# mLSTM heads: where the turned SSD columns, the second half's scaling and the output gate's tanh stand

## What is computed

```
y_ssd = group_rmsnorm((y + d_skip * xs) * silu(z), norm_w, SSD_GROUPS)   # 2 groups of 512 columns
qk    = silu(causal_dwconv_2(qk, conv_w, conv_b))                       # 4 taps, 2048 columns
h     = num / den, per head, then normed per head                      # 8 heads of 128
y_ml  = sigmoid(o_pre) * h
x     = x + concat([y_ssd, y_ml]) @ w_out
```

## Time and profile before

| | us |
|---|---|
| median of 3 runs (1051.25 to 1052.91) | 1052.33 |
| the profiled execution, its own time | 1052.15 |
| its span, from first to last instruction | 1050.4 |
| TensorE busy | 1024.9 (98% of the span) |
| VectorE busy | 844.0 (80%) |
| ScalarE busy | 665.8 (63%) |

### The profile page before, as it was taken

The page is one execution under the profiler, slowest core; times in us unless marked ns, Lnnn a source line. Parts: engine busy times, 40 slices in busy tenths (PEclk is TensorE's granted clock), DMA queues, the critical chain, the costliest instruction groups (busy, mean ns, idle before and its releaser), DMA issues. The chain is left out here.

```text
span 1050.4 us, 14956 instructions
## 1 busy us (share of the span) xinstructions
PE 1024.9 (98%) x5574; PEld 867.9 (83%) x5574; DVE 844.0 (80%) x1091; ACT 665.8 (63%) x833; POOL 33.2 (3%) x40
## 2 busy tenths in 40 slices
PE   7999999999999999999999999999999999999997
PEld 6778999999999788989878778787878787777775
DVE  5856776766777767887868799999999999999976
ACT  5554655555565746566544677777777777777754
POOL 1001000000000100100220000000000000000000
PEclk9999999999999999999999999999999999999998
DMA  9734447464624445333204889998989898999971
GB/s 343 266 121 140 148 174 231 144 227 156 206 85 161 160 163 164 121 123 120 81 33 182 316 322 379 358 385 347 389 349 387 348 385 349 370 364 373 364 281 43
DMA packets 82712, 253.61 MB, mean 241 GB/s; under 512 B 4161, under 2 KB 42177, under 8 KB 62657
## 3 DMA queue, kind: packets, MB, share of 16 engines
q1 hardware_dynamic: 82624, 252.50, 63.9%
HBM read 251.44 MB, written 1.05 MB: 240 GB/s over the span
## 5 line engine op out<-in xcount | busy, mean ns | idle before, releaser
L1061 DVE TENSOR_TENSOR WL<-raw,WH 128x2048 fp32r<-128x2048 f32 x232 | 497.8, 2176 | 95.6 <-ACT WH L544 95.5
L544 ACT ACTIVATE WH<-raw 128x2048 fp32r<-128x2048 f32 x232 | 421.5, 1823 | 91.3 <-PE bank L1991 75.7
L1989 PE MATMUL bank<-WH,MXH 128*128 128x512 f32 x552 | 218.8, 396 | 0.2 <-DVE WL L1061 0.2
L1991 PE MATMUL bank<-WH,MXL 128*128 128x512 f32 x552 | 215.4, 390 | 0.0
L1990 PE MATMUL bank<-WL,MXH 128*128 128x512 f32 x552 | 214.9, 389 | 0.0
L1989 PE MATMUL bank<-HTH,WH 128*128 128x256 f32 x576 | 165.3, 287 | 2.4 <-DVE HTL L1084 1.2
L1990 PE MATMUL bank<-HTL,WH 128*128 128x256 f32 x576 | 162.9, 283 | 0.0
L1991 PE MATMUL bank<-HTH,WL 128*128 128x256 f32 x576 | 162.9, 283 | 0.0
L1989 PE MATMUL bank<-WH,HTH 128*128 128x512 f32 x348 | 138.6, 398 | 3.3 <-DVE WL L1108 1.5
L1990 PE MATMUL bank<-WL,HTH 128*128 128x512 f32 x348 | 136.1, 391 | 0.0
L1991 PEld LDWEIGHTS bank<-WH,MXL 128*128 128x128 f32 x552 | 103.6, 188 | 22.4
(11 more groups left out here) (393 smaller groups left out, 1097.8 us busy)
## 6 DMA issues: line engine op xcount, KB each, us to landing
raw<-in_exp_w_up SPq DMA_DIRECT2D x52, 1024.0 KB, 7.4
raw<-in_exp_w_gate SPq DMA_DIRECT2D x52, 1024.0 KB, 8.1
raw<-in_exp_w_down SPq DMA_DIRECT2D x52, 1024.0 KB, 6.8
raw<-in_w_in SPq DMA_DIRECT2D x34, 1024.0 KB, 5.1
raw<-in_w_up SPq DMA_DIRECT2D x22, 1024.0 KB, 5.4
raw<-in_w_down SPq DMA_DIRECT2D x11, 1024.0 KB, 5.2
raw<-in_w_out SPq DMA_DIRECT2D x8, 1024.0 KB, 4.9
raw<-in_w_o SPq DMA_DIRECT2D x4, 1024.0 KB, 6.6
```

The lines of the kernel that those rows point to most:

```text
L544: e.activation(WH[i % HL][:, 0:n], raw[i % RAW][:, 0:n], ACT.Copy).then_inc(a_wh, 1)
L1061: e.tensor_tensor(l, r, h.bitcast(F32), ALU.subtract).then_inc(v_wl, 1)
L1989: e.matmul(out_, ah, bh, start=start, stop=False)
L1991: return e.matmul(out_, al, bh, start=False, stop=stop)
```

## The change

- **Column parts one head later.** The four `ssd_columns(n)` stood behind heads 0 to 3 as n = h; they now stand behind heads 1 to 4 as n = h - 1, on all three engines.
- **Scaling of the second group.** VectorE's `group_norm(1)` leaves its place ahead of the head loop and goes to `turned()` of head 2, ahead of the column part there.
- **Output gate.** The two halves' tanh on ScalarE stood in heads 1 and 2; they now stand in heads 0 and 2.

```diff
@@ scalar: turned() of the head loop
                     ml_turned(h)
-                    if h < 4:
-                        ssd_columns(h)
-                    if h in (1, 2):
+                    if 0 < h < 5:
+                        ssd_columns(h - 1)
+                    if h in (0, 2):
                         e.wait_ge(a_og, 4)
-                        e.activation(OG[:, h - 1, :], OG[:, h - 1, :], ACT.Tanh, scale=0.5).then_inc(a_ogt, 1)
+                        e.activation(OG[:, h // 2, :], OG[:, h // 2, :], ACT.Tanh, scale=0.5).then_inc(a_ogt, 1)
@@ vector: ahead of the head loop
             product("mk", 0, 1)
-            group_norm(1)
             split(PI["mk", 0] + 2)
@@ vector: turned() of the head loop
-                    if h < 4:
-                        ssd_columns(h)
+                    if h == 2:
+                        group_norm(1)
+                    if 0 < h < 5:
+                        ssd_columns(h - 1)
```

## The result

The changed kernel takes 1053.44 us (median of 20 runs, 1052.45 to 1054.64), the kernel before beside it on the same chip 1051.84 us (20 runs). The ratio is 1.0014, with a 95% interval of 1.0008 to 1.0020: 1.5 us slower, inside the 0.2% that the prediction called no change, and of the sign that it forecast (+1.3 us). The profiled execution took 1053.05 us, with a span of 1051.3; that is only 0.90 us more than the profiled execution before. The two differ elsewhere too: the kernel before has a fall of the granted clock near its end (0.66 from 1025 to 1030 us) that this execution has not.

The account below looks back on a forecast made before the run. TensorE, busy 98%, was taken as the bound. Gains reach -0.80 at ml_s(2), back to -0.11 at ml_s(4), then +0.45 for the part and +0.96 wait: +1.30, 1053.45 on the execution, median 1053.6, range 1051.4 to 1054.8.

Parts of the forecast that it names:

- What bounds: mLSTM stretch: TensorE has 1.70 us at most to win, no slack after 466 us; VectorE and ScalarE loop in equal steps.
- Scaling leaves the head of the loop: VectorE ahead of head 0: split, taps and sums come 0.80 us earlier; ml_s(2) runs at 464.53, still waiting 1.35 us.
- head 2 takes it back: VectorE behind head 2's tile 1 taps: the scaling spends the 0.80 us lead; head 3's taps stay at 473.65.
- The wait at ml_y(0): TensorE in head 0, just ahead of 450.19: a 0.26 us gap that goes away.
- slower: Rival, chance 0.14: head 0 never wins the 0.80 us lead but head 2 pays it; +2.10 us, median 1054.4.
- Column part leaves head 0: Head 0: VectorE wins nothing, as the part filled a wait for ScalarE; on TensorE 0.45 us is put off, not removed.
- Tanh: ScalarE: one 1.07 us gate tanh moves from head 1 into head 0's 2.23 us idle time, at no cost.
- ml_v(4): TensorE behind head 4: waits 0.96 us for VectorE's late read of the fourth column part; runs at 490.66, 1.30 us later.
- hand over: Between the end of VectorE's column read and ml_v(4): put at 0.15 us; without any, the lower bound is +1.06.
- Not slower: Rival, chance 0.14: VectorE's idle time absorbs the scaling in head 2, the 0.80 us lead lasts; median 1052.0, or 1052.8 execution.
- The rule of the Trainium skill: Speed up the engine blocking the matmul engine: by it alone, relieving the 1.44 us gap at ml_s(2) would be a gain.
- The clock: TensorE's clock is 1.00 around the 1.44 us gap; no new wait is longer, so no drop was expected.

Follow-up runs that it names:

- gn_home_fill: The changed kernel with the second group's scaling back ahead of the head loop, plus 5 idle matmuls ahead of ml_s(2): 1053.29 us against 1052.11 before.
- after_fill: The changed kernel with 5 idle matmuls on TensorE in the gap ahead of ml_s(2): 1053.19 us against 1052.05 for the kernel before.
- part3_late: The kernel before with only the fourth column part moved from behind head 3 to behind head 4, on all three engines: 1052.78 us against 1052.05.
- read_early_fill: The changed kernel, VectorE reading the last column part ahead of head 4's tile 1 taps, plus 5 idle matmuls ahead of ml_s(2): 1052.31 us against 1052.11.
- tanh_only: The kernel before with only the gate's first tanh moved from head 1 to head 0: 1051.87 us against 1052.11.
- gn_slot_fill: The changed kernel, scaling in head 0 behind the product of tile 0, plus 5 idle matmuls ahead of ml_s(2): 1052.72 us against 1052.11 before.
- slots: The kernel before with VectorE's scaling (head 0) and column reads (heads 1 to 4) each behind the product of tile 0: 1050.76 us against 1051.61.
- gn_home: The changed kernel with the second group's scaling back ahead of the head loop: 1054.15 us against 1051.61 for the kernel before.
- read_early: The changed kernel with VectorE reading the last column part in head 4 ahead of the taps of tile 1: 1052.71 us against 1051.61 before.
- gn_slot: The changed kernel with the scaling in head 0 behind the product of tile 0: 1053.30 us against 1051.61 for the kernel before.
- the filled kernels: The kernels before and after the change, each with 5 idle matmuls on TensorE ahead of ml_s(2): 1051.53 and 1053.19 us.
- before_fill: The kernel before with 5 idle matmuls on TensorE in the gap ahead of ml_s(2): 1051.53 us against 1052.05.

## Why the prediction was right, step by step

- **What bounds.** That VectorE's order within a head decides, and that TensorE has no slack behind 466 us, holds: each wait added or taken there showed in full at the turning of x (gn_home_fill and after_fill +1.24, part3_late +1.18, read_early_fill +0.25).
- **Scaling leaves the head of the loop, and head 2 takes it back.** ml_s(2) 0.81 us earlier, head 3's taps where they were, to 0.01 us. One term was too small: TensorE waited 1.48 us there and not 1.35. The wait at ml_y(0) was put at its row's 0.26 us, but the start came 450.19 - 449.65 = 0.54 us behind the matmul ahead of it, where the series steps by 0.12, so 0.42 us went with it. This changed nothing in the sum, as ml_s(2) waits for the product. gn_home_fill shows that its place makes no difference to the end. The rival "slower", a lead never won, is out: the first split is at 445.19 - 0.21 = 444.98.
- **Column part leaves head 0.** VectorE won nothing by it; in the profile after, VectorE's taps of head 1 follow those of head 0's tile 1 at the old 2.55 us (453.40 to 455.95; before 453.99 to 456.54), with a wait of 0.48 us for ScalarE where the column part stood. TensorE's 0.45 us per part gives its arrival at ml_v(4) to 0.03 us.
- **Tanh.** At no cost, as put: tanh_only.
- **ml_v(4).** The mechanism is right and its size nearly: predicted +1.30, measured +1.17 at ml_v(4) itself (490.53 against 489.36) and +1.22 at the turning of x. The term that was off is the hand over. I took 0.15 us from a product to its matmul; from the end of the column read (489.82 + 0.86 = 490.68) to ml_v(4) at 490.74 it was 0.06. The lower bound of the text, +1.06, had it at nothing. The wait itself has 0.72 us in its row against 0.96 put; that is mostly the same counting of idle time as at ml_y(0), and by starts it cost 0.86.
- **"Not slower".** Its premise was half right. The 1.38 us of idle does take up work, if it is put into it (gn_slot_fill, slots), but the change puts the work behind the taps, and there it comes on top, as the prediction said (the 0.80 us lead is gone at head 3's taps). And even with the lead kept the end is +0.47, since the last read stands too late in its head; the prediction had +0.50 for that.
- **The rule of the Trainium skill** (Perfetto Trace Analysis, optimization strategies: relieve what blocks the matmul engine) would have had a gain. This case's traces agree with the rule where the relief lasts: slots relieves VectorE in the whole loop, and the stretch is 0.99 us shorter. In the change the relief was a loan over two heads.
- **The clock.** "No new wait here is longer, so I expect no drop" was the weak step. The wait at ml_s(2) did get longer, 1.48 us instead of 1.44, and in three of the four profiles with 1.48 or 1.49 us there (gn_home, read_early and gn_slot, but not the changed kernel's own) the clock fell behind it; in the three with 1.43 or 1.44 us it did not. Seven profiles are too few to say that the length decides. The medians are 1.60 us apart and the stretches 1.22. That dips at ml_s(2) make the 0.4 is not shown, and the filled kernels speak against it, with 1.66 and 1.37; it is within the spread of the runs.
- **The number.** That the median came within 0.2 us of the 1053.6 put down is in part luck. The forecast stood on a median of three runs, 1052.33; twenty gave 1051.84. The medians moved by 1.60 and not by 1.3, and the two misses nearly cancel.

## What to carry to other kernels

Work moved out of the way of one wait has to be followed to the next instruction that waits for the same queue, and to the release of every buffer that it holds. Here 0.80 us gained at head 2 was spent by head 4, and a bank that had been free 7 us early became the bound. Look instead for the place inside the loop where the busy engine itself idles (here behind the product of tile 0, 1.38 us in each head): work put there was free for the scaling (0.79 us), and some 5 us later in a head, behind the taps of tile 1, it was not.

## What the runs showed that was not expected

- A wait of 1.48 us on TensorE can cost twice: of the seven profiles with an unfilled gap of 1.43 to 1.49 us at ml_s(2) (before, changed, gn_home, read_early, gn_slot, part3_late, tanh_only) three show that the granted clock fell to its lower level behind it, and the next 3.60 us of matmuls took 5.10 to 5.14. None of the six profiles with fillers there shows it, nor does slots with its gap of 0.88 us; with three dips in fourteen profiles that is a hint and no proof. What decides between falling and not falling is open. At the last unit the length alone does not decide it: there the clock fell behind 1.34 us in the kernel before, and stayed at 1.00 behind 1.91 us in after_fill:

```profile
1025.45 0.51 PE L1989 MATMUL bank<-WH,HTH 128*128 128x512 f32 x1 [1.34 <-DVE HTH L1858]
```
```profile
1026.95 0.50 PE L1990 MATMUL bank<-WH,HTH 128*128 128x512 f32 x1 [1.91 <-DVE HTH L1859]
```

- At the end of the stretch such a dip costs 0.90 us (read_early against read_early_fill), 1.35 (gn_slot) or 1.40 (gn_home): less than its 1.50 where a wait that follows takes up a part. In read_early it is the wait at ml_s(4), 0.68 us in read_early_fill and none with the dip.
- A dip appears also at 355 to 365 us (part3_late) and behind 1025 us (before, before_fill, and gn_home, which thus has two), so single executions of one kernel can differ by as much as this whole change. Differences of a microsecond were told apart here by the trace between two fixed instructions, not by the total time.
